# Hybrid decoder step on one core: first layer's token norms from rows of x, loads reordered, copies and small steps moved

## The chip, the cores and the metric

The kernel runs on one core of one Trainium2 chip. The metric is the device time of the whole program in microseconds (us), as a median of runs. Beside it stands one profiled execution, whose trace gives the rows below. TensorE is called PE here, its weight loads PEld, VectorE DVE, ScalarE ACT, GpSimd POOL and SyncE SP.

## The reference

Two layers of one mixer block over 512 prompt tokens and 8 sample tokens, width 1024, in float32:

```python
def mixer_layer(x, s0_re, s0_im, conv_buf, mk, mv, p):
    h = rmsnorm(x, p['norm_g'])
    u_a, z_a, u_b, z_b, q, z_x, g_a, g_b, g_x = jnp.split(h @ p['w_in'], IN_SPLITS, axis=-1)
    y_a, s_new = s5_branch(u_a, s0, ...)           # 32 groups x 64 complex states, scan over tokens
    ...                                            # GELU, half GLU, SiLU gate, projection: o_a
    v_b = u_b[..., :E_CONV] * jax.nn.sigmoid(u_b[..., E_CONV:])
    ...                                            # depthwise conv of 31, LayerNorm, gate: o_b
    ...                                            # attention into 256 memory tokens (mk, mv), gate: o_x
    m = jax.nn.sigmoid(g_a) * o_a + jax.nn.sigmoid(g_b) * o_b + jax.nn.sigmoid(g_x) * o_x
    x = x + (m @ p['w_out']).astype(x.dtype)
```

Here rmsnorm(x, g) is x * rsqrt(mean(x * x) + 1e-6) * g over the 1024 channels of a token. The memory keys and values mk, mv are rmsnorm(mem) @ w_k and @ w_v. A last rmsnorm ends the trunk, and states, conv buffers, keys and values are outputs too.

## The kernel before

The residual x lives transposed in SBUF as `xT` (channels on partitions, 8 tiles of 128 x 520: 512 prompt and 8 sample tokens in two halves of 260). Each engine has one hand-written program, in order, and semaphores tie them; `wait(eng, l, name, n)` waits in layer l for the n-th event of a name.

**Weights.** All of w_in, the branch weights and w_out pass through a ring of two slots `w_st` in 72 units of 512 KB a layer. For each unit SP issues a load (`ring_load`, L335), as soon as the slot's last unit has been split; ACT rounds it to `w_hi` (`high`, L1141), and the rest `w_lo` comes from a POOL subtraction (L613) or, for the units of `by_transfer`, from an ACT negation (L1140) and an adding DMA that POOL issues (L610). PE then makes three products per unit (`products`: L693 high by high, L699 the two mixed ones) into one of two PSUM accumulators `acc`, which ACT or DVE empties and frees (`acc_free`).

**Start.** SP issues, in this order: 11 small parameter rows (`parameter_rows`), two loads of memory rows `mrow`, the first of 8 key and value loads `kv_load` (three buffers `kvw`; load i from 3 on waits until load i-3 is used), the rows of x (`xrow`), two ring loads, 16 small state loads (`state_rows`), and then the other five kv_loads. PE turns parameters, memory rows and x rows (L658), makes keys and values in 8 steps (`key_values`, L735), and sums the squares of x over the channels with a matrix of ones (`sum_squares`, L748): ACT squares the 8 tiles of `xT` (L1099), DVE adds them up (L1569), PE sums over partitions, DVE scales and takes reciprocals over 128 x 520 (L1436, L1595), ACT the root (L1165) and `rs` is there. Then for each tile DVE scales it to `ht` (L1439), ACT rounds it to `h_hi` (L1168), DVE takes `h_lo` (L1601), and the first unit of layer 0 takes the tiles as they come.

**Inside a layer** PE goes through the units v, q, u, vb, zx, gx, zb, gb, za, ga, out, with attention, convolution (DVE, L1439), scans (DVE) and state products between them. What the change touches:
- `x_keep` stores xT to DRAM in four parts of 520 KB from SP's queue (L378), because `merge("gx", ...)` writes over xT; DVE waits for all four (`x_out`, L1874) before the first merge, and merges free the accumulators of the next gates (L1790).
- After the second scan `keep_states(1)` copies four blocks of X to X2 on DVE (L1843); PE's second state products (`outputs(1)`, L964) wait for it (L1845). In the first half DVE copies two blocks and ACT two (L1360).
- While the last 8 units of layer 0 (`out`) run, DVE adds each to xT (L1960), which frees its accumulator, and between them computes the next layer's state matrices: `powers` after the first add, `level_factors` after the second and third, and so on.

Of the kernel before, what the change touches and what calls it, by code (L numbers as in the profile page):

```python
# [21 lines left out]
P = 128  # L22
# [48 lines left out]
def build(nc, x_prompt, x_sample, mem_prompt, state_ssm_re, state_ssm_im, state_conv, cache_mem_k,  # L71
# [12 lines left out]
    with ctx:  # L84
# [54 lines left out]
        def rr(name, off, shape):  # L139
            return at(r_at, off, rlen, name, shape)  # L140
# [37 lines left out]
        msq = rr("msq", 7296, [P, D])  # L178
        kT = rr("kT", 6144, [P, HEADS, MEM])
# [74 lines left out]
            V2_done=2 X2_done=1 s_turned=2  # L254
# [10 lines left out]
        def wait(eng, l, name, value):  # L265

            eng.wait_ge(sm[name], l * per[name] + value)
# [50 lines left out]

        block = ctx.enter_context(nc.Block())
# [3 lines left out]
        def _(sp):  # L323
# [57 lines left out]
            def parameter_rows(l):  # L381
                sp.dma_start(dtrow[64:80, :], ssm_log_dt[l].rearrange("(q e) -> q e", e=2)).then_inc(sm["dt_in"], 16)
                rows = ((0, 16, ssm_a_re[l].rearrange("(q e) p -> q (e p)", e=2)),
                        (16, 4, b_glu[l].rearrange("(k p) -> k p", p=P)),
                        (20, 4, conv_b[l].rearrange("(k p) -> k p", p=P)),
                        (24, 4, conv_ln_g[l].rearrange("(k p) -> k p", p=P)),
                        (28, 4, conv_ln_b[l].rearrange("(k p) -> k p", p=P)),
                        (32, 16, ssm_a_im[l].rearrange("(q e) p -> q (e p)", e=2)),
                        (48, 8, norm_g[l].rearrange("(k p) -> k p", p=P)),
                        (56, 8, mem_norm_g[l].rearrange("(k p) -> k p", p=P)))  # L390
                for r0, n, src in rows:
                    sp.dma_start(prow[r0:r0 + n, :], src).then_inc(sm["p_in"], 16)
                sp.dma_start(cwrow[:, :], conv_w[l].rearrange("k (i c) -> (k i) c", c=P)).then_inc(sm["p_in"], 16)
                sp.dma_start(drow[:, :], ssm_d[l].rearrange("(q x) -> q x", x=P)).then_inc(sm["p_in"], 16)

# [44 lines left out]
            parameter_rows(0)  # L440
# [3 lines left out]
            kv_load(0, 0)  # L444
            kv_load(0, 1)
# [5 lines left out]
            sp.dma_start(xsrow[:, :], x_sample[:, 0, :]).then_inc(sm["xs_in"], 16)  # L451
            value_loads(0, "v", 0)
            state_rows(0)

            for l in range(LAYERS):
                for i in range(3, 8):
                    kv_load(l, i)
# [8 lines left out]
                in_loads(l, "q", 5 * E, 3, 4)  # L466
                cache_load(l, 1)
# [11 lines left out]
                if l == 0:  # L479
                    sp.wait_ge(sm["x_ev"], 5)  # L480
                else:
                    sp.wait_ge(sm["x_sum"], l * KT)
                x_keep(0, 2)
# [24 lines left out]
                x_keep(4, 6)  # L508
# [46 lines left out]
                if l + 1 < LAYERS:  # L555
                    wait(sp, l, "br_a_done", 4)
                    parameter_rows(l + 1)
# [98 lines left out]
        def _(pe):  # L656
# [122 lines left out]
            key_values(0, 4, 5)  # L779
# [5 lines left out]
            key_values(0, 5, 7)  # L785
            pe.wait_ge(sm["x_ev"], 5)
            sum_squares(0)
            key_values(0, 7, 8)
            state_parameters(0)

            for l in range(LAYERS):
# [155 lines left out]
                def outputs(f):  # L947
# [13 lines left out]
                    if f == 0:  # L961
                        wait(pe, l, "X2_done", 1)
# [128 lines left out]
        def _(act):  # L1091
# [18 lines left out]

            discretise(0)
# [13 lines left out]
            for i in range(4):  # L1125
# [16 lines left out]

            high(0)
            high(1)
            for l in range(LAYERS):
# [172 lines left out]

                gate("gx", 0)
# [38 lines left out]
                wait(act, l, "x_scan", 1)  # L1358
                for ri in range(2):
                    last = act.copy(X2[ri * S:(ri + 1) * S, :, 1, :], X[S:2 * S, ri, :, 0:YC])  # L1360
                last.then_inc(sm["X2_done"], 1)
# [10 lines left out]
                wait(act, l, "br_b_done", 4)  # L1372
                silu("za", 0, q)
# [54 lines left out]
        def _(dve):  # L1428
# [66 lines left out]
            def powers(l):  # L1495

                wait(dve, l, "par_act", 1)
# [3 lines left out]
                tt(pw[:, 1, :, 1], tiny[:, 3, :], tiny[:, 7, :], ALU.mult)  # L1501

# [13 lines left out]
                for lo in (1, 2, 4):  # L1516
                    a = tiny[:, 0:lo, :].rearrange("p k q -> p q k")
                    b = tiny[:, 4:4 + lo, :].rearrange("p k q -> p q k")
                    cmul(pw[:, 0, :, lo + 1:2 * lo + 1], pw[:, 1, :, lo + 1:2 * lo + 1], pw[:, 0, :, 1:lo + 1], pw[:, 1, :, 1:lo + 1],
                         pw[:, 0, :, lo:lo + 1].to_broadcast([P, Q, lo]), pw[:, 1, :, lo:lo + 1].to_broadcast([P, Q, lo]), a, b)  # L1520
# [66 lines left out]
            for k in range(1, KT):  # L1587
                add_square(0, k)
            steps.clear()

            for l in range(LAYERS):

                wait(dve, l, "sq_used", 1)
                ts(rs[:, :, :], mp[:, 0:2, 0:HC], 1.0 / D, EPS, ALU.mult, ALU.add)
                dve.reciprocal(rs[:, :, :], rs[:, :, :]).then_inc(sm["var_done"], 1)  # L1595

                wait(dve, l, "rstd_done", 1)

# [239 lines left out]
                def keep_states(f):  # L1838

                    qs = slice(f * QH, (f + 1) * QH)  # L1840
                    for e in range(f + 1):
                        for ri in range(2):
                            run(dve.tensor_copy(X2[ri * S:(ri + 1) * S, :, e, :], X[e * S:(e + 1) * S, ri, :, 0:YC]), behind=2 * e + ri)  # L1843
# [109 lines left out]
                merge("ga", 3)  # L1953
                steps.clear()

                for i in range(KT):
# [69 lines left out]
```

## Time and profile before

| | us |
|---|---|
| median of 3 runs (1249.85 to 1251.44) | 1251.43 |
| the profiled execution | 1245.38 |
| its span, first to last instruction | 1243.6 |
| PE busy in the span | 1119.2 |
| DVE busy | 729.0 |
| ACT busy | 479.8 |
| POOL busy | 245.1 |

The span lies 1.8 us below the time of its execution, and that execution 6.0 us below the median of the runs. Busy times overlap; a stage is read from the wait that ends last in it.

### The profile page before, as it was taken

Reading aid. Unit: us, or ns where it says so; the run is one execution under the profiler, and the core shown is the slowest. Engines: PE = TensorE matmul, PEld = TensorE weight load, DVE = VectorE, ACT = ScalarE, POOL = GpSimd, SP = SyncE. Lnnn points to the kernel's source line nnn. Section 1 sums busy time; section 2 is a strip of 40 time slices with the busy share of each in tenths; the row PEclk is TensorE's granted clock in tenths of the full one; section 3 lists DMA queues with packets and bytes.
Section 4 is the critical chain, followed back from the end, with each engine's and each line's share of the span. In section 5 each row is a group of like instructions: output and inputs, shape, how many; then the busy total and the mean of one; then the engine's idle time right before and its main releaser. Section 6 shows DMA issues by size and latency. Waiting matters only on the chain.

```text
span 1243.6 us, 20132 instructions
## 1 busy us (share of the span) xinstructions
PE 1119.2 (90%) x8266; PEld 1040.1 (84%) x8266; DVE 729.0 (59%) x1229; ACT 479.8 (39%) x646; POOL 245.1 (20%) x183
## 2 busy tenths in 40 slices
PE   5679999889999989998889999988999998899895
PEld 3359996788999979998865999678999898899895
DVE  4289965637678660545875766664557864133412
ACT  3233563434463622233123356343446362222112
POOL 0114111111110122243330411120111012124430
PEclk9779998989998998998899999898999898899998
DMA  8405878897765576173222588888876557424332
GB/s 234 118 12 162 215 200 241 221 154 155 171 136 122 137 158 120 57 231 117 64 88 85 149 224 205 237 228 150 168 156 135 124 139 156 90 66 138 108 109 76
DMA packets 217873, 181.98 MB, mean 146 GB/s; under 512 B 47146, under 2 KB 187882, under 8 KB 216998
## 3 DMA queue, kind: packets, MB, share of 16 engines
q1 hardware_dynamic: 205542, 135.61, 39.8%
q0 software_dynamic: 12096, 44.05, 19.4%
q8 instruction: 65, 1.06, 0.3%
q10 hardware_dynamic: 144, 1.05, 0.2%
q14 instruction: 26, 0.21, 0.1%
HBM read 121.86 MB, written 15.72 MB: 111 GB/s over the span
## 4 chain that ended last, share of the span: by engine, by line
PE 59%; DVE 17%; DMA 11%; SPq 6%; ACT 4%; issue 3%; DVEq 0%; POOL 0%; ACTq 0%
PE acc L699 31%; PE acc L693 15%; DMA w_lo<-w_st 5%; PE acc L1057 2%; DMA w_st<-in_w_in 2%; PE acc L735 2%; PE mp L964 2%; PE mp L658 1%; DVE cacc L1439 1%; ACT w_lo L1140 1%; SPq L514 1%; DVE xT L1433 1%; PE mp L929 1%; PE mp L832 1%; PE mp L867 1%
## 5 line engine op out<-in xcount | busy, mean ns | idle before, releaser
L699 PE MATMUL acc<-h_hi,w_lo 128*128 128x260 f32 x1664 | 341.0, 287 | 9.4 <-DMA w_lo<-w_st 9.4
L699 PE MATMUL acc<-h_lo,w_hi 128*128 128x260 f32 x1664 | 338.0, 285 | 0.0
L699 PEld LDWEIGHTS acc<-h_hi,w_lo 128*128 128x128 f32 x1664 | 261.0, 192 | 10.4 <-DMA w_lo<-w_st 10.4
L699 PEld LDWEIGHTS acc<-h_lo,w_hi 128*128 128x128 f32 x1664 | 261.0, 192 | 0.0
L1141 ACT CAST w_hi<-w_st 128x1024 fp32r<-128x1024 f32 x144 | 149.6, 1040 | 280.8 <-PE acc L699 244.3
L693 PE MATMUL acc<-h_hi,w_hi 128*128 128x260 f32 x1664 | 238.0, 297 | 19.3 <-DVEq L1602 10.9
L693 PEld LDWEIGHTS acc<-h_hi,w_hi 128*128 128x128 f32 x1664 | 219.3, 198 | 29.5 <-DVEq L1602 11.7
L613 POOL TENSOR_TENSOR w_lo<-w_st,w_hi 128x1024 fp32r<-128x1024 f32 x60 | 150.5, 2510 | 400.8 <-ACT w_hi L1141 400.8
L1140 ACT ACTIVATE w_lo<-w_st 128x1024 fp32r<-128x1024 f32 x84 | 89.1, 1060 | 304.9 <-PE acc L699 213.8
L610 POOL DMA_DIRECT2D w_lo<-w_st x84 | 73.0, 868 | 562.4 <-ACT w_lo L1140 552.8
L1439 DVE SCALAR_TENSOR_TENSOR cacc<-vx,cw,cacc 128x512 f32<-128x512 f32 x232 | 161.7, 767 | 3.6 <-DVE xT L1433 1.7
L699 PE MATMUL acc<-bh,w_lo 128*128 128x260 f32 x384 | 80.4, 292 | 9.6 <-DMA w_lo<-w_st 9.6
L1433 DVE TENSOR_TENSOR sg<-acc,sg 128x520 f32<-128x520 f32 x32 | 22.4, 699 | 111.5 <-PE acc L699 108.4
L735 PE MATMUL acc<-kvw,memg 128*128 128x512 f32 x128 | 62.6, 646 | 12.8 <-DMA kvw<-in_w_k 9.0
L699 PEld LDWEIGHTS acc<-bh,w_lo 128*128 128x128 f32 x384 | 62.0, 197 | 10.6 <-DMA w_lo<-w_st 10.6
L693 PE MATMUL acc<-bh,w_hi 128*128 128x260 f32 x384 | 58.0, 293 | 11.1 <-DVEq L1911 4.2
L735 PEld LDWEIGHTS acc<-kvw,memg 128*128 128x128 f32 x128 | 26.2, 209 | 44.3 <-issue 33.3
L693 PEld LDWEIGHTS acc<-bh,w_hi 128*128 128x128 f32 x384 | 51.5, 195 | 13.7 <-issue 5.3
L699 PE MATMUL acc<-m_hi,w_lo 128*128 128x260 f32 x256 | 54.9, 298 | 0.0
L699 PE MATMUL acc<-m_lo,w_hi 128*128 128x260 f32 x256 | 54.2, 295 | 0.0
L699 PE MATMUL acc<-q_r,w_hi 128*128 128x260 f32 x256 | 51.5, 283 | 0.0
L693 PE MATMUL acc<-m_hi,w_hi 128*128 128x260 f32 x256 | 36.3, 295 | 14.8 <-DVEq L1961 7.5
(282 smaller groups left out, 1397.4 us busy)
## 6 DMA issues: line engine op xcount, KB each, us to landing
w_st<-in_w_in SPq DMA_DIRECT2D x104, 512.0 KB, 4.7
w_lo<-w_st POOLq DMA_DIRECT2D x84, 512.0 KB, 5.5
kb<-in_cache_mem_k SPq DMA_DIRECT2D x16, 512.0 KB, 5.8
kb<-in_cache_mem_v SPq DMA_DIRECT2D x16, 512.0 KB, 7.0
w_st<-in_w_out SPq DMA_DIRECT2D x16, 512.0 KB, 4.0
x_scratch<-xT SPq DMA_DIRECT2D x8, 520.0 KB, 6.1
xT<-x_scratch SPq DMA_DIRECT2D x4, 1040.0 KB, 8.0
kvw<-in_w_k SPq DMA_DIRECT2D x8, 512.0 KB, 6.1
```

Of the source, the lines that this page charges most:

```text
L514: sp.dma_start(Ug[t * H:(t + 1) * H, :, NB:NB + C], ug[:, :, t // 4, (t % 4) * C:(t % 4 + 1) * C]).then_inc(sm["U_in"], 16)
L610: pool.dma_start(w_lo[:, n % 2, :], w_st[:, n % 2, :], accum_op=ALU.add).then_inc(w_lo_done[n % 2], 16)
L613: pool.tensor_tensor(w_lo[:, n % 2, :], w_st[:, n % 2, :], w_hi[:, n % 2, :].bitcast(F32), ALU.subtract).then_inc(w_sub_done, 1)
L693: pe.matmul(acc_ps[acc][:, a, 0:HC], w_of(w_hi, n % 2, k), high[:, k, a, :], start=(k == 0), stop=False)
L699: last = pe.matmul(acc_ps[acc][:, a, 0:HC], w_of(w, n % 2, k), x[:, k, a, :], start=False, stop=(k == kts - 1 and w is w_hi))
L735: last = pe.matmul(acc_ps[half][:, m, :], memg[:, k, m * P:(m + 1) * P], kvw[:, i % 3, kk * E:(kk + 1) * E], start=(k == 0), stop=(k == KT ...
L964: last = pe.matmul(mp[:, 2 * e + r // 4, (r % 4) * YC:(r % 4 + 1) * YC], V2[:, r, e, :], X2[:, r, e, :], start=False, stop=(r % 4 == 3))
L1057: last = pe.matmul(acc_ps[j][:, a, 0:HC], w_dir[:, g, k * 2 * P + j * P:k * 2 * P + (j + 1) * P], u[:, k, a, :], start=(k == 0), stop=(k = ...
L1140: act.activation(w_lo[:, n % 2, :], w_st[:, n % 2, :], ACT.Copy, scale=-1.0).then_inc(w_neg_done, 1)
L1141: act.copy(w_hi[:, n % 2, :], w_st[:, n % 2, :]).then_inc(w_hi_done, 1)
L1433: run(dve.tensor_tensor(out, a, b, op), behind)
L1439: run(dve.scalar_tensor_tensor(out=out, in0=a, scalar=s, in1=b, op0=op0, op1=op1), behind)
```

## The change

1. **Start, loads.** Five parameter rows are issued by ACT, six by SP, and these after the memory rows and the first kv_load. x_sample's rows are loaded after x's first block. kv_loads 3 to 5 come ahead of the state loads.
2. **Start, norm of layer 0.** ACT squares rows of x (and x_sample) with a sum over the row as it goes; DVE turns the five columns of sums into reciprocals and multiplies them into diagonal matrices `diag`, `sdiag`; PE multiplies ones by these, which spreads each token's value over all partitions; ACT takes the root from PSUM as `rs`. The squares of xT's tiles, their sums and the wide reciprocal of layer 0 go. PE turns x_sample's rows ahead of kv step 4 and makes the spread after it, where the sum came after step 6. PE turns the parameters after the first block of memory rows.
3. **x_keep** stands earlier in SP's order: the first part after unit q 3, the second where the first was, the others after vb and zx units.
4. **keep_states(1)** copies two blocks; ACT copies the other two (`states_turned(1)`), ahead of `silu("za", 0)`.
5. **powers** of layer 1 is cut in three, and the first two parts run ahead of the adds of `out`; a level moves from the second to the third add.

```diff
+        diag = rr("diag", 8320, [P, 4, P])
+        sdiag = rr("sdiag", 8832, [NB, NB])
...
 # SP
-            parameter_rows(0)
...
             kv_load(0, 0)
+            parameter_rows(sp, 0, 5)
             kv_load(0, 1)
...
                 if i == 0:
                     kv_load(0, 2)
-            sp.dma_start(xsrow[:, :], x_sample[:, 0, :]).then_inc(sm["xs_in"], 16)
+                    sp.dma_start(xsrow[:, :], x_sample[:, 0, :]).then_inc(sm["xs_in"], 16)
+            kv_load(0, 3)
             value_loads(0, "v", 0)
+            kv_load(0, 4)
+            kv_load(0, 5)
             state_rows(0)
...
-                for i in range(3, 8):
+                for i in range(3 if l else 6, 8):
...
                 in_loads(l, "q", 5 * E, 3, 4)
+                if l == 0:
+                    sp.wait_ge(sm["x_ev"], 5)
+                else:
+                    sp.wait_ge(sm["x_sum"], l * KT)
+                x_keep(0, 2)
                 cache_load(l, 1)
...
-                x_keep(0, 2)
+                x_keep(2, 4)
...
                 value_load(l, "vb", 3, 1)
-                x_keep(2, 4)
+                x_keep(4, 6)
                 in_loads(l, "zx", 6 * E, 0, 1)
+                x_keep(6, 8)
...
                 gate_loads(l, "gx", 2, 4)
-                x_keep(4, 6)
...
-                gate_loads(l, "gx", 4, 5)
-                x_keep(6, 8)
-                gate_loads(l, "gx", 5, 7)
+                gate_loads(l, "gx", 4, 7)
 # PE
-            parameters(0)
             for m in range(2):
                 pe.wait_ge(sm[f"mem_in{m}"], 16)
                 if m:
+                    parameters(0)
                     wait(pe, 0, "par_ev", 1)
...
-            key_values(0, 5, 7)
+            key_values(0, 4, 5)
             pe.wait_ge(sm["x_ev"], 5)
-            sum_squares(0)
-            key_values(0, 7, 8)
+            wait(pe, 0, "sq_summed", KT - 1)
+            for i in range(4):
+                pe.matmul(mp[:, i // 2, (i % 2) * P:(i % 2 + 1) * P], ones[:, :], diag[:, i, :], start=True, stop=True)
+            for a in range(2):
+                last = pe.matmul(mp[:, a, 4 * C:HC], ones[0:NB, :], sdiag[:, 4 * a:4 * a + 4], start=True, stop=True)
+            last.then_inc(sm["sq_used"], 1)
+            key_values(0, 5, 8)
...
-                    if f == 0:
-                        wait(pe, l, "X2_done", 1)
+                    wait(pe, l, "X2_done", f + 1)
 # ACT
+            parameter_rows(act, 0, 0, 5)
...
+            def square_row(i, rows, row):
+                act.wait_ge(sm["xs_in"] if i == 4 else sm[f"x_in{i}"], 16 if i == 4 else 32)
+                steps.run(act.activation(msq[0:rows, :], row, ACT.Square, accum_out=stat[0:rows, 16 + i:17 + i]))
+                act.sem_inc(sm["sq_done"], 4 if i == 4 else 1)
+
+            square_row(0, P, xrow[:, 0, :])
+            square_row(4, NB, xsrow[:, :])
+            for i in range(1, 4):
+                square_row(i, P, xrow[:, i, :])
...
-            for k in range(KT):
-                square(0, k)
...
                 if l == 0:
+                    wait(act, l, "sq_used", 1)
+                    act.activation(rs[:, :, :], mp[:, 0:2, 0:HC], ACT.Sqrt).then_inc(sm["rstd_done"], 1)
                     keep_keys(0, ktok)
-                    wait(act, l, "var_done", 1)
-                    act.activation(rs[:, :, :], rs[:, :, :], ACT.Sqrt).then_inc(sm["rstd_done"], 1)
...
                 wait(act, l, "br_b_done", 4)
+                states_turned(1)
                 silu("za", 0, q)
 # DVE
             powers(0)
-            for k in range(1, KT):
-                add_square(0, k)
+            wait(dve, 0, "sq_done", KT)
+            ts(stat[:, 21:25], stat[:, 16:20], 1.0 / D, EPS, ALU.mult, ALU.add, behind=1)
...
+            run(dve.reciprocal(stat[:, 26:30], stat[:, 21:25]), behind=1)
...
+            for i in range(4):
+                run(dve.tensor_scalar(diag[:, i, :], ident[:, :], stat[:, 26 + i:27 + i], None, ALU.mult), behind=i + 1)
+            run(dve.tensor_scalar(sdiag[:, :], ident[0:NB, 0:NB], stat[0:NB, 30:31], None, ALU.mult))
...
-                    for e in range(f + 1):
-                        for ri in range(2):
-                            run(dve.tensor_copy(X2[ri * S:(ri + 1) * S, :, e, :], X[e * S:(e + 1) * S, ri, :, 0:YC]), behind=2 * e + ri)
+                    for ri in range(2):
+                        run(dve.tensor_copy(X2[ri * S:(ri + 1) * S, :, 0, :], X[0:S, ri, :, 0:YC]), behind=ri)
...
                 merge("ga", 3)
+                if l + 1 < LAYERS:
+                    first_powers(l + 1)
+                    input_factors(l + 1)
...
-                            powers(l + 1)
+                            for lo in (1, 2, 4):
+                                more_powers(lo)
                         elif i == 1:
-                            level_factors(l + 1, 0, 3)
+                            level_factors(l + 1, 0, 2)
                         elif i == 2:
-                            level_factors(l + 1, 3, 5)
+                            level_factors(l + 1, 2, 5)
```

## Rows read from the trace of the kernel before

**Rows 1.** The page: engines' busy time; x_keep's DMAs (KB each, us to landing).

```profile
PE 1119.2 (90%) x8266; PEld 1040.1 (84%) x8266; DVE 729.0 (59%) x1229; ACT 479.8 (39%) x646; POOL 245.1 (20%) x183
...
x_scratch<-xT SPq DMA_DIRECT2D x8, 520.0 KB, 6.1
```

**Rows 2.** PE's waits, whole run: for whom, us in total, times, longest.

```profile
PE acc L735 <- DMA kvw<-in_w_k: 9.0, 1, 9.0
PE acc L693 <- DVEq L1790: 8.4, 3, 4.7
PE mp L964 <- DVEq L1845: 7.9, 2, 4.0
PE acc L693 <- DVEq L1961: 7.5, 3, 5.4
```

**Rows 3.** Timeline of the start: start us, us, instruction, [idle before <-releaser].

```profile
4.81 0.84 SPq L443 DMA_DIRECT2D mrow<-in_mem_prompt  x2
...
6.98 0.37 PE L658 MATMUL mp<-ident,prow 80*128 80x80 f32 x1 [6.98 <-DMA drow<-in_ssm_d]
...
8.14 3.86 PE L658 MATMUL mp<-ident,mrow 128*128 128x128 f32 x16 [0.39 <-DMA mrow<-in_mem_prompt]
...
14.53 8.80 PE L735 MATMUL acc<-kvw,memg 128*128 128x512 f32 x16 [2.53 <-DVE memg L1580]
...
14.66 1.06 ACT L1119 ACTIVATE msq<-mrow 128x1024 f32<-128x1024 f32 x1
...
24.04 3.60 PE L735 MATMUL acc<-kvw,memg 128*128 128x512 f32 x8
...
51.03 9.73 DVE L1569 TENSOR_TENSOR sq<-sq 128x520 f32<-128x520 f32 x7 [23.85 <-ACT sq L1099]
...
67.25 0.64 ACT L1165 ACTIVATE rs<-rs 128x520 f32<-128x520 f32 x1 [2.85 <-DVE rs L1595]
```

**Rows 4.** The chain that ended last, whole run: start us, us, what.

```profile
33.48 4.03 DMA kvw<-in_w_k
...
82.72 5.75 PE acc L699 x32
...
90.38 3.83 PE acc L699 x32
...
465.59 6.92 PE mp L964 x32
...
983.95 3.76 PE mp L964 x32
```

**Rows 5.** PE, timeline around the first merges of layers 0 and 1.

```profile
259.24 1.91 PE L658 MATMUL mp<-ident,wt 128*128 128x128 f32 x16
265.88 3.81 PE L693 MATMUL acc<-h_hi,w_hi 128*128 128x260 f32 x16 [4.73 <-DVEq L1790]
...
856.41 3.81 PE L693 MATMUL acc<-h_hi,w_hi 128*128 128x260 f32 x16 [3.55 <-DVEq L1790]
```

**Rows 6.** ACT there in layer 0; then stretches: us, busy by engine, PE clock, DMA share, GB/s.

```profile
265.58 1.92 ACT L1287 COPY wl<-mp 128x1024 f32<-128x1024 f32 x2
...
105.00:110.00 5.00, 5.00 (x44) 5.00 (x43) 4.52 (x15) 1.66 (x4) 2.21 (x1) 1.00 0.70 212
...
15.00:20.00 5.00, 5.00 (x9) 2.11 (x8) 2.89 (x18) 4.03 (x7) 0.00 (x0) 0.66 1.05 313
```

**Rows 7.** DVE, timeline of the adds of out, layer 0 (columns as in rows 3).

```profile
590.15 0.70 DVE L1433 TENSOR_TENSOR xT<-acc,xT 128x520 f32<-128x520 f32 x1 [6.83 <-PE acc L699]
...
591.41 2.53 DVE L1433 TENSOR_TENSOR pw<-tiny 128x16 f32<-128x16 f32 x2
...
596.79 0.41 DVE L1433 TENSOR_TENSOR tiny<-pw 128x16 f32<-128x16 f32 x2
```

**Rows 8.** Copies to X2 in layer 0, and POOL's subtractions beside them, by timeline.

```profile
459.20 5.98 DVE L1843 COPY X<-X 64x576 f32<-64x576 f32 x4
...
459.32 5.06 POOL L613 TENSOR_TENSOR w_lo<-w_st,w_hi 128x1024 fp32r<-128x1024 f32 x2 [8.41 <-ACT w_hi L1141]
```

More of the change, by code:

```diff
@@ L317, in g3, with parameter_rows @@
             return ap[:, :, :, 0:4 * C]
+        def parameter_rows(eng, l, first=0, end=11):
+            if first == 0:
+                eng.dma_start(dtrow[64:80, :], ssm_log_dt[l].rearrange("(q e) -> q e", e=2)).then_inc(sm["dt_in"], 16)
+            rows = ((0, 16, ssm_a_re[l].rearrange("(q e) p -> q (e p)", e=2)),
+                    (16, 4, b_glu[l].rearrange("(k p) -> k p", p=P)),
+                    (20, 4, conv_b[l].rearrange("(k p) -> k p", p=P)),
+                    (24, 4, conv_ln_g[l].rearrange("(k p) -> k p", p=P)),
+                    (28, 4, conv_ln_b[l].rearrange("(k p) -> k p", p=P)),
+                    (32, 16, ssm_a_im[l].rearrange("(q e) p -> q (e p)", e=2)),
+                    (48, 8, norm_g[l].rearrange("(k p) -> k p", p=P)),
+                    (56, 8, mem_norm_g[l].rearrange("(k p) -> k p", p=P)))
+            for r0, n, src in rows[max(first - 1, 0):end - 1]:
+                eng.dma_start(prow[r0:r0 + n, :], src).then_inc(sm["p_in"], 16)
+            if end < 11:
+                return
+            eng.dma_start(cwrow[:, :], conv_w[l].rearrange("k (i c) -> (k i) c", c=P)).then_inc(sm["p_in"], 16)
+            eng.dma_start(drow[:, :], ssm_d[l].rearrange("(q x) -> q x", x=P)).then_inc(sm["p_in"], 16)
         block = ctx.enter_context(nc.Block())
@@ L1124, in _, with high @@
             act.wait_ge(sm["mem_rt"], 1)
+            def high(n):
+                if n < LAYERS * UNITS:
+                    act.wait_ge(w_loaded[n % 2], (n // 2 + 1) * 16)
+                    if by_transfer(n):
+                        act.activation(w_lo[:, n % 2, :], w_st[:, n % 2, :], ACT.Copy, scale=-1.0).then_inc(w_neg_done, 1)
+                    act.copy(w_hi[:, n % 2, :], w_st[:, n % 2, :]).then_inc(w_hi_done, 1)
+            def square_row(i, rows, row):
[6 more added lines that the diff above has]
+                square_row(i, P, xrow[:, i, :])
             for i in range(4):
@@ L1130, in _ @@
             act.activation(xT[:, :, :, 4 * C:HC], mp[:, 0, 0:KT * NB].rearrange("p (k a c) -> p k a c", a=2, c=4), ACT.Copy).then_inc(sm["x_ev"], 1)
-            for k in range(KT):
-                square(0, k)
             steps.clear()
-            def high(n):
-                if n < LAYERS * UNITS:
-                    act.wait_ge(w_loaded[n % 2], (n // 2 + 1) * 16)
-                    if by_transfer(n):
-                        act.activation(w_lo[:, n % 2, :], w_st[:, n % 2, :], ACT.Copy, scale=-1.0).then_inc(w_neg_done, 1)
-                    act.copy(w_hi[:, n % 2, :], w_st[:, n % 2, :]).then_inc(w_hi_done, 1)
             high(0)
@@ L1317, in turned_outputs, with states_turned @@
                     last.then_inc(sm["V2_done"], 1)
+                def states_turned(f):
+                    wait(act, l, "x_scan", f + 1)
+                    for ri in range(2):
+                        last = act.copy(X2[ri * S:(ri + 1) * S, :, 1, :], X[S:2 * S, ri, :, 0:YC])
+                    last.then_inc(sm["X2_done"], 1)
                 gate("gx", 0)
@@ L1357, in _ @@
                 gate("gb", 2)
-                wait(act, l, "x_scan", 1)
-                for ri in range(2):
-                    last = act.copy(X2[ri * S:(ri + 1) * S, :, 1, :], X[S:2 * S, ri, :, 0:YC])
-                last.then_inc(sm["X2_done"], 1)
+                states_turned(0)
                 gelu_outputs(0)
@@ L1840, in keep_states @@
                     qs = slice(f * QH, (f + 1) * QH)
-                    for e in range(f + 1):
-                        for ri in range(2):
-                            run(dve.tensor_copy(X2[ri * S:(ri + 1) * S, :, e, :], X[e * S:(e + 1) * S, ri, :, 0:YC]), behind=2 * e + ri)
+                    for ri in range(2):
+                        run(dve.tensor_copy(X2[ri * S:(ri + 1) * S, :, 0, :], X[0:S, ri, :, 0:YC]), behind=ri)
                     run(dve.tensor_copy(sf[:, :, qs], X[:, :, :, XC - 1]))
@@ L1964, in _ @@
                         if i == 0:
[L1965 removed]
+                            for lo in (1, 2, 4):
+                                more_powers(lo)
                         elif i == 1:
[L1967 removed]
+                            level_factors(l + 1, 0, 2)
                         elif i == 2:
[L1969 removed]
+                            level_factors(l + 1, 2, 5)
                         elif i == 3:
```

49 lines of the change are left out of this document (20 added, 29 removed).

## The prediction

> **What bounds the kernel now.** I read the page first: PE is busy for 1119 of 1243.6 us [rows 1], so a gain can only come from stretches where PE stands still or runs at its lower clock. The list of PE's waits gives the places [rows 2]: a key load at the start, the merges of gx (L1790), the second state products (L964), the adds of `out` (L1961). The timeline of each place gives the size. At the start PE sets little: the fourth key step waits for a load that was issued at 33.48 only, behind the small state loads [rows 4], and the norm of x is a long chain of DVE work (7 adds over 9.73 us, later a wide reciprocal) before the root at 67.25 [rows 3]; layer 0's first unit ends at 82.72 + 5.75 = 88.5 [rows 4]. By then the 8 key steps, at 3.6 us when PE doesn't wait [rows 3], could have been over for 30 us. The reader is to see that this stretch is set by order, not by work.
>
> **Edits 1 and 2, the start.** I work out when the first unit ends.
>
> Keys begin at 14.53 now, when both blocks of memory rows are turned, copied and scaled [rows 3]. Their loads were issued at 4.81 and the first was there at 8.14, 3.3 us later; they now go out first, at about 0.7. But PE turns the parameters ahead of the second block, and six parameter rows are issued behind two memory blocks and a key load, 1.5 MB. At the 313 GB/s of a full stretch [rows 6] 512 KB take 1.7 us, so in order of issue these rows land at 0.7 + 3.3 + 2 x 1.7 = 7.4 plus their own 1 to 2.5 us, against 6.98 now [rows 3]. Taken at 8.9, with an estimated 1.6 us for their turns and copies (6.98 to 8.14 is 1.2, and a little is left after it) and the 4.4 us from the second block's turns (halfway through the 3.86 us after 8.14, at 10.1) to 14.53, keys begin at 14.9. Were the rows to land as soon as now after their issue (2.6 us after some 4 us of issues), keys would begin at 12.5; the other bound is 16.5, with all of the queue ahead of them and 2.6 us more. I take 15.0, since no row shows a small load passing a large one.
>
> The Trainium skill ("DMA: Bandwidth & Descriptors", Queues, rings and completion order) says that a DMA engine takes the descriptors of one ring in order, which speaks against putting parameters behind 1.5 MB: by it 15.0, and 1202.9 at the end; without it 12.5 and 1200.4. The same page (Issuing engines are not separate DMA queues) says that the five rows on ACT save issue time alone. No row of this trace shows a parameter load on ACT's queue.
>
> From there PE's order is: two key steps and x block 0, 9.5 us (14.53 to 24.04); key step 2, 3.6; x block 1, 1.0 (half of a memory block's 1.9, which ran at the lower level); step 3, 3.6; two x blocks, 2.0; x_sample 0.7 (estimate, smaller than a block); step 4, 3.6; the spread, 0.9 (estimate; from 0.4, half a block, to 2) [rows 3]. That is 24.9, so the root starts at 39.9 instead of 67.25.
>
> From the root to the end of the high products 15.5 us pass now (67.25 to 82.72), bound by DVE's two steps per tile, and they stay. The next steps on ACT, two copies of keys, fall in DVE's first tile and cost some 0.2. But POOL's two first subtractions now fall about here: one that meets a DVE step costs it 2.1 us (two steps took 2.53 at 591.41 and the same two 0.41 at 596.79 [rows 7]). I take 1.3, between 0 and 2.1. High products then end at 56.7. By PE's count alone (three more key steps from 39.9) it would be free at about 52, so the tiles decide. The mixed products take 3.83 after a busy PE and 5.75 after a waiting one [rows 4]; I take 4.6: 61.3. **Gain 27.2**, bounds 19 (keys at 16.5, spread 2, collision 2.1, 5.75, a key load late by its 4.0) and 32.
>
> The Trainium skill ("SBUF — State Buffer", Who interferes with whom) has the rule for the collision: VectorE with two SBUF inputs and a GpSimd step that reads SBUF lock each other out for a whole instruction. By it the term is up to a whole subtraction, 2.5 us (5.06 for two in [rows 8]) instead of 1.3, and the sum 1.2 us later.
>
> At nothing I cost: the five row squares on ACT, 5 x 1.25 (1.06 [rows 3] and an estimated 0.2 for the sum), from about 20 to 27, hidden because PE asks for the first x copy at 15 + 9.5 + 3.6 + 1.0 + 3.6 = 32.7 (uncovered, up to 6 us); DVE's nine small steps, done by about 30, asked for at 39; the key loads. Load 3 is issued when step 0 is over, at 19.4, lands in 4.0 and is wanted at 29; SP waits there, and behind it stand the ring loads, which ACT wants only at 36. Loads 6 and 7 come after the state loads, as load 3 did; I see about 2 us of slack, and a late one costs at most 4.0 [rows 4].
>
> **Edit 3, the stores.** PE stands still before gx's third gate for 4.73 and 3.55 us, since DVE's first merge waits for the last store, and the gate's first block then runs in 3.81 [rows 5]. A block's 16 products at the higher level take half, 1.9, so 1.9 more goes each time. Gone: 6.6 in layer 0, 5.4 in layer 1. Next late are ACT's `wl` copies, over at 267.5 [rows 6]; the gate would run from 261.2 (259.24 + 1.91) for 1.9 + 3.83 to 266.9, so the state products wait half a microsecond, not seven. On SP the third and fourth stores leave the place ahead of U's loads and the ring loads of gx, and all parts now go ahead of loads in the q, vb and zx units. There the DMA engines are busy to 0.70 (105 to 110) [rows 6], so a store fits; bounds are 0 and 1.7 us (520 KB at 313 GB/s) for three stores a layer, 10 in all. I take 1.0, near the first, by the free share. **Gain 11.0**, bounds 2 and 12.
>
> **Edit 4, X2.** DVE's four copies in layer 0 take 5.98 beside POOL's two subtractions [rows 8]; PE waits 7.9 us in the two layers [rows 2], and the products after it take 6.92 instead of 3.76 [rows 4]. With two copies left, the second still meets POOL's first subtraction in layer 0 and ends at about 462.3, 3.0 earlier; if PE's pause then is short enough, up to 3.2 more. In layer 1 one copy pair saves 1.0; and ACT now does its copies before it splits unit za 2, so POOL's subtraction of that unit comes after the scan and 2.1 of collision leave it. Bounds are 1.0 and 6.2 in each layer; I take 3.0 and 4.0. The new wait on ACT for the scan holds `silu("za", 0)`, that split and the GELU tables; PE wants them after its state products and unit za 1, over 9 us later (3.76 + 5.75), so it is hidden; uncovered it costs what the scan is late. What follows, y through DRAM, starts with the products and moves with them. **Gain 7.0.**
>
> **Edit 5, powers.** DVE sits idle for 6.83 us before the first add [rows 7]. The steps from 591.4 to 596.8, 5.4 us, move into that pause. 2.1 of them are a collision, which meets another step instead, since POOL still has one subtraction per unit and DVE stays the bound. **Gain 3.3**, bounds 1.5 and 5.4. The level that goes to the third add is the same work.
>
> **Sum.** 27.2 + 11.0 + 7.0 + 3.3 = 48.5: the profiled 1245.4 would be 1196.9, and, as that execution lies 6.0 below the median of the runs, the median 1202.9.
>
> **Rivals.** *The start pays less*, because a load is late: parameters behind still more of the queue, or keys behind ring loads of many short rows. For it speaks that SP's order is the whole edit and that a key load was the longest wait; against it the slack above. With 8 us lost the time is 1211. *The stores give nothing*: the merge goes earlier, but state products wait for U's loads or `wl`, late by the same DMAs. For it speaks 267.5 being only 0.6 after 266.9; against it that x's stores leave that stretch. Gain 2 instead of 11: 1212. *Slower*: the stores move into the stream of weights, and each delays a unit by its whole landing, 6.1 us [rows 1]. Eight of them cost 49 and edit 3 gives nothing: 1251.4 - 37.5 + 49 = 1263. It decides from 37.5 / 8 = 4.7 us a store; against it the DMA share of 0.70, and that one store stood among the vb units already. *Nothing happens*: the norm isn't what the first unit waits for; the rows at 67.25 and 82.72 speak against it.
>
> **Numbers.** Forecast 0.72, less at the start 0.12, no gain from the stores 0.11, slower 0.02, nothing 0.02, the rest between. The range takes in the first two rivals on one side and most of the good bounds (32 + 12 + 10 + 5 = 59) on the other: 1191 to 1219. A measurement of this kernel tells some 0.2%, 2.5 us, from no change: faster 0.96, same 0.02, slower 0.02.
>
> **What would show it.** Layer 0's first mixed products near 57 instead of 82.7, the root near 40, no wait of PE for a key load. No wait of PE for L1790 before gx's third gate, and that block in 1.9. L964's wait under 1.5 us at least once. The add of tile 6 some 3 us sooner after the add of tile 0. Wrong I'd be if keys began past 18, if PE's waits for `w_lo` or `w_st` grew by more than 10 us in the q to zx units, or if PE's mean clock fell.

## The result: 1200.9 us, 0.959 of the time before

The changed kernel takes 1200.88 us (median of 4 runs, 1198.69 to 1206.69) against 1251.43 before; the ratio is 0.9594, 95% interval 0.9553 to 0.9636. A second set of six runs, beside experiments below, gave 0.9623 (0.9593 to 0.9652). Where a single part is taken away I compare with the mean of the two, 0.961, good to some 0.0025 (3 us). The profiled execution takes 1202.02 us, 43.4 less than the one of before; its mean granted clock is 0.963 instead of 0.944. The second set has a profiled execution too (1199.59 us), called the second execution below. The forecast was 1203, and 48.5 us of gain.

### The profile after

The page's rows for the engines' busy time and for the stores answer to [rows 1]:

```profile
PE 1107.5 (92%) x8274; PEld 1032.2 (86%) x8274; DVE 713.0 (59%) x1225; ACT 483.1 (40%) x652; POOL 246.6 (21%) x183
...
x_scratch<-xT SPq DMA_DIRECT2D x8, 520.0 KB, 5.3
```

PE's waits over the whole run (for whom, us in total, times, longest) answer to [rows 2]:

```profile
PE acc L706 <- DMA w_lo<-w_st: 23.6, 12, 4.4
PE acc L700 <- DVEq L1841: 6.9, 2, 3.5
...
PE acc L700 <- DVEq L2007: 4.9, 3, 2.7
...
PE mp L974 <- ACT X L1342: 3.6, 4, 1.3
```

The key load is gone from the list, and so is L1834 (L1790 before), the merge that frees an accumulator. L974 holds all state products: the second ones, which waited 7.9 us for VectorE, have 2.3 of its 3.6, now for ScalarE. L2007 (the adds of `out`) is down from 7.5 to 4.9. L1841 (L1797 before, 7.3 us) is the end of the last merge, for which the first unit of `out` waits in each layer (the first at 553); it has changed little. The row for `w_lo`, a weight's low part that a DMA makes, was 18.9 before: some of the gain goes there.

The start, by the timeline, answers to [rows 3, 4]:

```profile
0.74 0.88 SPq L447 DMA_DIRECT2D mrow<-in_mem_prompt  x2
...
8.54 0.37 PE L665 MATMUL mp<-ident,prow 80*128 80x80 f32 x1 [2.14 <-DMA drow<-in_ssm_d]
...
14.67 9.16 PE L742 MATMUL acc<-kvw,memg 128*128 128x512 f32 x16 [2.54 <-DVE memg L1614]
...
28.84 3.60 PE L742 MATMUL acc<-kvw,memg 128*128 128x512 f32 x8
...
40.19 0.60 ACT L1183 ACTIVATE rs<-mp 128x520 f32<-128x520 f32 x1 [2.90 <-PE mp L797]
...
55.29 0.40 PE L706 MATMUL acc<-h_hi,w_lo 128*128 128x260 f32 x2
...
59.13 1.13 PE L700 MATMUL acc<-h_hi,w_hi 128*128 128x260 f32 x8
```

The root starts at 40.19 instead of 67.25. Mixed products run from 55.29 to 59.13 (the next unit's start), 3.84 us, where before they ran from 82.72 for 5.75: the first unit is over 29 us sooner.

How the lead grows and shrinks is seen by taking the same instruction of PE in the profiles of both kernels (starts in us; the last row is the span; the last column is the lead of the second execution):

| instruction | before | after | lead | lead, second execution |
|---|---|---|---|---|
| second unit, layer 0 (the first is over) | 88.31 | 59.13 | 29.2 | 27.9 |
| first unit behind the first softmax | 154.36 | 128.17 | 26.2 | 26.8 |
| products of U, layer 0 (behind gx's third gate) | 274.10 | 240.57 | 33.5 | 33.6 |
| first glu product, layer 0 (behind y) | 492.82 | 461.69 | 31.1 | 31.2 |
| keys of layer 1 (`out` is over) | 642.24 | 606.16 | 36.1 | 34.9 |
| products of U, layer 1 | 864.62 | 823.70 | 40.9 | 39.4 |
| first glu product, layer 1 | 1088.64 | 1046.26 | 42.4 | 45.9 |
| end | 1243.6 | 1200.2 | 43.4 | 45.8 |

So the lead falls in two stretches: up to the first softmax, by 3.0 in one execution and 1.1 in the other, and between the products of U and glu in layer 0, by 2.4 in both, although the state copies of edit 4 lie in that stretch. In the others it grows or holds.

**The first softmax.** Timelines of VectorE (end of the first unit's tiles; the first probabilities) and of PE there, after:

```profile
54.98 0.42 DVE L1497 COPY s<-mp 128x256 f32<-128x256 f32 x1
...
122.68 1.22 DVE L1457 TENSOR_TENSOR pr<-pr,stat 128x1024 f32<-128x1024 f32 x1
...
124.02 1.44 PE L665 MATMUL mp<-ident,pr 128*128 128x128 f32 x8 [1.87 <-DVEq L1676]
125.25 3.27 PE L843 MATMUL mp<-kT,q 128*128 128x256 f32 x8
```

and before:

```profile
81.95 0.42 DVE L1473 COPY s<-mp 128x256 f32<-128x256 f32 x1
...
149.35 1.22 DVE L1433 TENSOR_TENSOR pr<-pr,stat 128x1024 f32<-128x1024 f32 x1
...
151.95 1.03 PE L658 MATMUL mp<-ident,pr 128*128 128x128 f32 x8
152.82 1.89 PE L832 MATMUL mp<-kT,q 128*128 128x256 f32 x8
```

VectorE needs 67.4 us from the tiles to the probabilities before (149.35 - 81.95) and 67.7 after: it works for 64 of them, through state inputs, level factors and a convolution. Its own lead is 27.0, PE's was 29.2; PE waits 1.87 for it and its next eight products then take 3.27 instead of 1.89. The lead above VectorE's is gone. In the second execution PE comes as VectorE is done, and both the wait and the slow products are missing:

```profile
125.05 1.09 PE L665 MATMUL mp<-ident,pr 128*128 128x128 f32 x8
125.98 1.89 PE L843 MATMUL mp<-kT,q 128*128 128x256 f32 x8
```

The products of U stand at 240.57 in the one and at 240.48 in the other. So a loss of this size belongs to one execution, and by the products of U it is no longer seen.

**The stores, state copies and adds.** PE at gx's third gate and its products of U in layer 0, and at the gate in layer 1 [rows 5]:

```profile
234.20 2.15 PE L700 MATMUL acc<-h_hi,w_hi 128*128 128x260 f32 x16
...
240.57 3.76 PE L940 MATMUL mp<-U,wl 128*128 128x72 f32 x32 [0.38 <-ACT wl L1306]
...
817.87 2.16 PE L700 MATMUL acc<-h_hi,w_hi 128*128 128x260 f32 x16
```

No wait and no slow block. The state copies and products in layer 0, and the products in layer 1 [rows 8]:

```profile
433.41 1.36 ACT L1342 COPY X<-X 64x576 f32<-64x576 f32 x2 [7.46 <-DVEq L1880]
...
433.41 0.94 DVE L1886 COPY X<-X 64x576 f32<-64x576 f32 x2
...
434.91 6.78 PE L974 MATMUL mp<-X,V 128*128 128x72 f32 x32 [1.28 <-ACT X L1342]
...
1018.74 6.91 PE L974 MATMUL mp<-X,V 128*128 128x72 f32 x32 [1.05 <-ACT X L1342]
```

The copies run side by side on two engines and end 1.4 us after the scan; the wait is 1.28 and 1.05 us, but the products still run slowly, 6.78 and 6.91 (6.44 and 5.71 in the second execution) instead of the 3.76 of a stretch at the upper clock [rows 4]. VectorE's adds of `out` for tiles 0 and 6, after [rows 7]:

```profile
557.50 0.70 DVE L1457 TENSOR_TENSOR xT<-acc,xT 128x520 f32<-128x520 f32 x1 [0.80 <-PE acc L706]
...
605.35 0.70 DVE L1457 TENSOR_TENSOR xT<-acc,xT 128x520 f32<-128x520 f32 x1
```

Before, tile 6 was added at 641.43, 51.3 after tile 0; now it is 47.9. The idle time ahead of the first add shrank from 6.83 to 0.80: the moved steps fill it.

### The profile page after: what moved, and what is told of

Its sections match the earlier page's. It is cut to its first block, busy times and chain, and to the rows that moved or that the text cites. A ratio compares the mean times of both kernels' runs of the same rounds, so it can differ in the third digit from the quotient of the medians.

```text
span 1200.2 us, 20152 instructions
## 1 busy us (share of the span) xinstructions
PE 1107.5 (92%) x8274; PEld 1032.2 (86%) x8274; DVE 713.0 (59%) x1225; ACT 483.1 (40%) x652; POOL 246.6 (21%) x183
## 4 chain that ended last, share of the span: by engine, by line
PE 53%; DVE 18%; DMA 14%; ACT 4%; SPq 3%; issue 2%; DVEq 0%; POOL 0%; ACTq 0%
PE acc L706 28%; PE acc L700 13%; DMA w_lo<-w_st 8%; DMA w_st<-in_w_in 4%; DVE cacc L1463 3%; PE acc L1067 2%; PE mp L974 2%; DVE wt L1457 2%; ACT w_lo L1142 2%; DVE tiny L1457 1%; PE mp L665 1%; PE acc L742 1%; PE mp L878 1%; PE mp L843 1%; DMA y_scratch<-U 1%
## 5 line engine op out<-in xcount | busy, mean ns | idle before, releaser
L700 PE MATMUL acc<-h_hi,w_hi 128*128 128x260 f32 x1664 | 231.8, 292 | 4.4 <-DVEq L1646 4.4
L700 PEld LDWEIGHTS acc<-h_hi,w_hi 128*128 128x128 f32 x1664 | 214.8, 194 | 12.7 <-issue 6.4
L742 PE MATMUL acc<-kvw,memg 128*128 128x512 f32 x128 | 58.5, 613 | 3.6 <-DVE memg L1614 2.5
L706 PE MATMUL acc<-m_lo,w_hi 128*128 128x260 f32 x256 | 52.2, 286 | 0.0
```

The lines of the kernel that those rows point to most:

```text
L700: pe.matmul(acc_ps[acc][:, a, 0:HC], w_of(w_hi, n % 2, k), high[:, k, a, :], start=(k == 0), stop=False)
L706: last = pe.matmul(acc_ps[acc][:, a, 0:HC], w_of(w, n % 2, k), x[:, k, a, :], start=False, stop=(k == kts - 1 and w is w_hi))
L742: last = pe.matmul(acc_ps[half][:, m, :], memg[:, k, m * P:(m + 1) * P], kvw[:, i % 3, kk * E:(kk + 1) * E], start=(k == 0), stop=(k == KT ...
```

## The experiments

All ratios are to the kernel before, run alongside; in brackets their 95% intervals. Each kernel but two starts from the changed one.

### Start alone, the rest alone

The kernel before with edits 1 and 2 only.

> The kernel before with the new start alone (edits 1 and 2). As predicted: 1251.4 - 27.2 = 1224 us, with layer 0's first unit over at about 59 us of the span. Rival, PE's gain is cut by VectorE's own backlog at the first softmax (there the changed kernel waits 1.9 us and runs slow after it, and its lead falls from 31.2 to 26.0 us): the end shows about 25 to 26, that is 1226. Rival, the start pays some 8 less: 1232.

Measured: 0.9799 [0.9772, 0.9827], a gain of 25.2 us. That excludes the start paying 8 less and can't tell 27.2 from 25 or 26; PE's first transposes of probabilities stand at 123.76 there, no sooner than in the changed kernel (124.02), but hardly wait:

```profile
123.76 1.09 PE L666 MATMUL mp<-ident,pr 128*128 128x128 f32 x8 [0.28 <-DVEq L1677]
124.69 1.89 PE L844 MATMUL mp<-kT,q 128*128 128x256 f32 x8
```

PE's lead over the kernel before is 27.8 at the second unit and 28.1 behind the softmax, so the rival's 25 to 26 may be the time, but its mechanism is not seen in this profile. The lead goes later: it is 28.0 at the products of U and 22.7 at the first glu product, for PE waits 3.80 us at 421 for the `w_lo` of gb's last unit (0.93 before) and 2.47 for y from DRAM (0.95 before). The lead of 31.2 in the expectation should be the 29.2 of the table. The rest alone, on the old start (edits 3 to 5):

> The kernel before with its old start and with the moves of stores, state copies and powers (edits 3 to 5). As predicted: 1251.4 - 21.3 = 1230 us. If the parts help each other (the start's lead is partly lost at the first softmax without them), start only and rest only sum to less than the 50.6 us of both; if one hides the other they sum to more.

Measured: 0.9829 [0.9803, 0.9855], a gain of 21.4 us, the forecast being 21.3. The sum of both, 46.6, stands beside 48.9 for both at once (0.039 of 1253), give or take 6: no sign that the halves help or hide each other.

### Stores back

```diff
-                x_keep(0, 2)
...
-                x_keep(2, 4)
...
+                x_keep(0, 2)
...
-                x_keep(4, 6)
+                x_keep(2, 4)
...
-                x_keep(6, 8)
...
                 gate_loads(l, "gx", 2, 4)
+                x_keep(4, 6)
...
-                gate_loads(l, "gx", 4, 7)
+                gate_loads(l, "gx", 4, 5)
+                x_keep(6, 8)
+                gate_loads(l, "gx", 5, 7)
```

> The changed kernel with the stores of x alone put back to their old places. As predicted (edit 3 is worth 11.0): about 1212 us, and PE stands still again for some 4 us before gx's third gate in both layers, with that gate's first block in 3.8 us. Rival, the stores give nothing because other loads are late anyway: 1203 (2 us). Rival, the two stretches are worth what they show in the traces (gains of 8.0 and 9.9 us around the third gate) and the stores cost nothing where they stand now: 1219. If the stores slow the weight loads they now stand among, PE's waits for w_lo (23.6 us in the changed kernel) fall by some us here.

Measured: 0.9727 [0.9693, 0.9761], 14.6 us (give or take 5) slower than 0.961; the profiled execution, 1212.2, is 10.2 above that of the changed kernel. PE's timeline has the two waits and the two slow blocks again:

```profile
237.79 3.81 PE L701 MATMUL acc<-h_hi,w_hi 128*128 128x260 f32 x16 [4.51 <-DVEq L1835]
...
828.37 3.80 PE L701 MATMUL acc<-h_hi,w_hi 128*128 128x260 f32 x16 [4.43 <-DVEq L1835]
```

So "the stores give nothing" is out; the forecast's 11 and the 18 of the third theory both lie within the interval. By the timelines of PE, the stretch from the first unit behind the softmax to layer 0's products of U takes 119.8 us here and 112.4 and 113.0 in the changed kernel's two executions, and that from the keys of layer 1 to its products of U 224.6 against 217.5 and 217.9: some 7 us in each layer, 14 in all. `w_lo`'s waits fall to 18.2 us, which could mean that the stores slow those weights where they stand now. The next kernel tests that.

### Stores of 4 KB

```diff
-                sp.dma_start(x_dram[:, first * w:end * w],
...
+                sp.dma_start(x_dram[:, first * w:first * w + 8],
+                             xT[:, first, 0, 0:8]).then_inc(sm["x_out"], 16)
```

> The changed kernel with stores of x of 8 columns of one tile each, in the same places with the same waits, and with what is read back taken from the weights in place of the stored x: it leaves out the bytes of the residual. If the stores cost what was predicted where they stand now (1.0 us for all): 1200 us, w_lo's waits unchanged at 23 us. If they are behind the growth of PE's waits for w_lo from 18.9 to 23.6 us: 1196 us, with some 5 us less of these waits.

Measured: 0.9615 [0.9577, 0.9653], the changed kernel's own time, and the row of PE's waits is where it was:

```profile
PE acc L706 <- DMA w_lo<-w_st: 23.2, 12, 4.0
```

The time alone, good to some 6 us, can't exclude the second theory's 5; the row does: without the bytes the waits are the same. The bytes of eight stores, 4 MB, cost nothing that can be measured here. The changed kernel beside it:

> The changed kernel once more, beside the three others of this group: 1201 us (1197 to 1206).

Measured: 0.9623 [0.9593, 0.9652], 1207.82 us (1199.59 to 1209.01), with 21.6 us of waits for `w_lo`. The median lies just outside what I wrote; the kernel before was 1254.63 in this group.

### The halves of the start

The changed kernel with the old norm (edit 2 undone):

> The changed kernel with edit 2 undone: the new load order with the old norm (squares of the turned tiles, seven adds of VectorE, a wide reciprocal). By the prediction's steps x is turned at 35, the squares end near 44, the adds near 46 and the root comes 6.5 us behind them as before, at 52.6 instead of 40.2: 12.4 us later than the changed kernel, 1213 us. Rival, the order of the loads carries the whole gain: 1201 to 1203. Rival, the norm carries nearly all of it: 1222 or more.

Measured: 0.9696 [0.9672, 0.9719], 10.8 us slower than 0.961 (give or take 4). With the old order of the loads instead (edit 1 undone):

> The changed kernel with edit 1 undone: the old load order with the new norm. Key load 3 stands behind the state loads again and lands near 37.5 where PE wants it at 28.8; the spread stands behind that key step, so the root comes 8.7 us later, at 49: 1210 us. Rival, the norm carries the whole gain: 1201 to 1203. If both parts are needed, the two alone leave less of the 27 us than their sum: 14.8 and 18.5.

Measured: 0.9726 [0.9696, 0.9756], 14.5 us slower (give or take 5). Root of the first, then key step 3 and root of the second, by the timeline:

```profile
51.88 0.64 ACT L1178 ACTIVATE rs<-rs 128x520 f32<-128x520 f32 x1 [2.85 <-DVE rs L1623]
```

```profile
40.80 5.66 PE L739 MATMUL acc<-kvw,memg 128*128 128x512 f32 x8 [10.48 <-DMA kvw<-in_w_k]
...
54.20 0.60 ACT L1179 ACTIVATE rs<-mp 128x520 f32<-128x520 f32 x1 [2.90 <-PE mp L794]
```

The first came as worked out (52.6 forecast). In the second the key load lands 3.3 us later than forecast and its step then runs slowly (5.66 instead of 3.60), so the root is at 54 and not at 49. Each half carries a part of the start, and neither the whole. The loads' order alone leaves 25.2 - 10.8 = 14.4 us and the norm alone 25.2 - 14.5 = 10.7, together 25.1: no sign that one needs the other.

### State copies back, powers back

```diff
 # ACT
-                states_turned(1)
...
 # DVE
-                    for ri in range(2):
...
+                    for e in range(f + 1):
+                        for ri in range(2):
```

> The changed kernel with edit 4 undone: VectorE makes all copies of the states. As predicted 7.0 us slower than the changed kernel (3.0 in layer 0, 4.0 in layer 1), that is 0.967 to 0.968 of the kernel before, and PE waits again near 4 us for VectorE before each second state product. Rival, ScalarE's copies only take the wait over: under 2 us.

Measured: 0.9664 [0.9638, 0.9691], 6.8 us slower (give or take 5). PE's second state products:

```profile
435.60 7.07 PE L975 MATMUL mp<-X,V 128*128 128x72 f32 x32 [3.90 <-DVEq L1889]
...
1026.76 7.07 PE L975 MATMUL mp<-X,V 128*128 128x72 f32 x32 [4.12 <-DVEq L1889]
```

The waits of before are back, 2.6 and 3.1 us longer than with ScalarE's help. For the powers `first_powers` and `input_factors` go back behind the first add:

> The changed kernel with edit 5 undone: the powers in one piece behind the first add. As predicted 3.3 us slower, 1.5 to 5.4, and the add of tile 6 comes 3 us later behind the add of tile 0. Rival, nothing: the memory keys of layer 1 start when their loads and scaled rows are there, and an earlier end of the adds is lost before them.

Measured: 0.9607 [0.958, 0.9633]. In time nothing is seen; the interval allows up to some 4 us. The timeline shows the edit at its place, the adds of tiles 0 and 6 standing 51.4 us apart instead of 47.9:

```profile
558.59 0.70 DVE L1457 TENSOR_TENSOR xT<-acc,xT 128x520 f32<-128x520 f32 x1 [7.00 <-PE acc L706]
...
609.94 0.70 DVE L1457 TENSOR_TENSOR xT<-acc,xT 128x520 f32<-128x520 f32 x1
```

PE's keys of layer 1 move with the adds: they start 52.2 us behind tile 0's add (at 610.76), 48.7 in the changed kernel (at 606.16). So the rival's reason is out, though the time doesn't show the 3.5 us.

### The wait at the first softmax

```diff
-                    level_factors(0, 0, 5)
...
                 convolution(2, 0, c1)
+                if l == 0:
+                    level_factors(0, 0, 5)
```

> The changed kernel with layer 0's level factors (12.9 us of VectorE from 74.0 to 86.9) moved behind the four softmaxes. If VectorE's backlog is what holds the first softmax, PE's wait of 1.9 us at 124 and the 1.6 us lost at the lower clock after it are gone: some 3 to 5 us sooner than the changed kernel, 1196 to 1198. Rival, the weights' loads or ScalarE end last there anyway: 1200 to 1201, with a wait for w_lo or for an accumulator in place of the one for VectorE.

Measured: 0.9616 [0.9589, 0.9642]: no gain is seen, and up to 4 us are not excluded. PE in u's first unit, at the softmax, and at the first glu product:

```profile
106.86 0.51 PE L706 MATMUL acc<-h_hi,w_lo 128*128 128x260 f32 x2 [2.02 <-DMA w_lo<-w_st]
...
124.48 1.04 PE L665 MATMUL mp<-ident,pr 128*128 128x128 f32 x8
125.35 1.89 PE L843 MATMUL mp<-kT,q 128*128 128x256 f32 x8
...
461.76 4.70 PE L1067 MATMUL acc<-u,w_dir 128*128 128x260 f32 x10 [2.53 <-DMA u<-y_scratch]
```

VectorE has the probabilities ready 5.5 us before PE comes, so its backlog is out of the way. But PE comes no sooner, at 124.48 against 124.02 and 125.05 in the changed kernel's two executions; it has waited 2.02 us for a `w_lo`, as the rival says (1.11 and 2.10 there). The products run in 1.89, which they also do in the second execution without this edit. And the glu product, which needs y back from DRAM, starts at 461.76, where the changed kernel has 461.69 and 461.60, after waits for that DMA of 2.53, 0.50 and 2.33 us. So whatever is won at the softmax is gone by glu.

### Two units split by GpSimd

```diff
-  return unit["q"] + 2 <= n % UNITS < unit["za"]
+  return unit["q"] + 2 <= n % UNITS < unit["za"] and n % UNITS not in (unit["gx"] + 1, unit["gb"] + 11)
```

> The changed kernel with two weight units a layer (gx unit 1 and gb unit 11) split by GpSimd's subtraction instead of the transfer that PE waits for (3.2 and 3.8 us in layer 0, 2.8 and 4.4 in layer 1). If the lead over the loads is what ends last there, PE's waits for w_lo fall from 23 to some 10 us and the kernel gains 6 to 10 us: 1192 to 1195. Rival, the next unit's weight is late by the same DMAs or the subtractions slow VectorE: under 3 us.

Measured: 0.9512 [0.9485, 0.9538], 1194.18 us: 12 us (give or take 5) better than the changed kernel, and the best of all. PE's waits for `w_lo`, and the one near gx:

```profile
PE acc L706 <- DMA w_lo<-w_st: 14.3, 9, 3.2
```

```profile
209.35 0.51 PE L706 MATMUL acc<-h_hi,w_lo 128*128 128x260 f32 x2 [3.21 <-DMA w_lo<-w_st]
```

The waits for gb's last unit, 3.78 us at 418 and 4.38 at 1002 (3.75 and 2.20 in the second execution), are gone, and no other took over at their place; y's way through DRAM cost more, though (6.9 us of waits in all, 1.7 and 4.5 before the edit). The second state products behind them took 5.13 and 3.76, so some more may have come from the clock. Whether the whole gain is that of this unit is not shown, for both units were changed at once. In gx I had the wrong unit: PE still waits there, so the late transfer is that of unit 0. Whether splitting that one pays more was not tried.

The same kernel with the late factors, and with all parameter rows on ScalarE's queue:

> The kernel with two units split by GpSimd, layer 0's level factors behind the softmaxes, and all parameter rows on ScalarE's queue. If a queue's own order held the six rows back, they land 2.6 us after their issue, near 7.8 instead of 8.5, and keys start some 0.7 us sooner; if the DMA engines' order holds them wherever they are issued, they land at 8.5 or later. In time 3 us below the kernel with the two units alone if the softmax's wait counts at the end, the same if the transfer of y through DRAM takes it back.

Measured: 0.9576 [0.9552, 0.96], 8 us worse than the two units alone. The timeline shows why (the last row's issue; the parameters and the keys on PE):

```profile
5.49 0.69 ACTq L337 DMA_DIRECT2D drow<-in_ssm_d  x1
...
19.21 0.37 PE L664 MATMUL mp<-ident,prow 80*128 80x80 f32 x1 [13.08 <-DMA drow<-in_ssm_d]
...
25.33 9.44 PE L741 MATMUL acc<-kvw,memg 128*128 128x512 f32 x16 [2.54 <-DVE memg L1613]
```

The rows were there 13 us after their issue, and keys begin at 25.33 instead of 14.67. By 5.49 SP had issued 3.0 MB (memory, three key loads, the first block of x). Another 1.5 MB, the other blocks of x, followed. Up to 19.0 us the two queues had moved (packets, MB, busy share; q1 is SP's queue, q10 ScalarE's):

```profile
q1 hardware_dynamic: 1677, 4.51, 90.7%
q10 hardware_dynamic: 296, 0.10, 3.3%
```

That is more than the 3.0 MB, so most of what was issued later went ahead of the rows too. Both of my theories fail: a queue of its own neither lets the rows pass nor keeps them in the order of issue. At the end the kernel has made up for some of the 10.7 us; how much of that the late factors give stays open.

## Why the prediction was right

**Start, 27.2 forecast.** Measured 25.2 in time (22 to 29), 29.2 at the first unit's end. Keys 15.0, found 14.67; root 39.9, found 40.19; mixed products 56.7, found 55.29, since GpSimd's two subtractions were over by 41.1, when VectorE's tiles had hardly begun: the 1.3 us for the collision were not paid. They took 3.84, not 4.6. Nine profiles, those of the experiments included, have this start: keys begin at 14.67 to 16.08 (so the bound of 12.5, rows that pass large loads, is out), the mixed products take 3.84 or 5.37, and the second unit starts at 59.1 to 60.7 instead of the forecast's 61.3, a lead of 27.6 to 29.2. So the steps came as worked out. Two slips carry no weight: the 0.2 us for the copies of keys is not in the 56.7, and the bound of 16.5 for the keys is 16.0 by the numbers given for it (7.4 + 2.6 + 1.6 + 4.4).

What I had put at nothing is what becomes of the lead behind the first unit. VectorE's backlog of setup, 67 us long, meets PE at the first softmax; it takes back 3.0 us in the profiled execution, 1.1 in the second and none with the start alone. More goes before layer 0's glu, 5.3 us with the start alone, where the `w_lo` of gb's last unit and y are late next. Against the time of the kernel these are small, so the sum holds; that it holds to 2 us is partly luck.

**Stores, 11.0.** Measured 14.6 (10 to 19) in time and 10.2 in the profiled executions. Both waits and both slow blocks went, as counted, and the lead grows by 7.3 and 4.8 us over these stretches (6.6 and 5.4 forecast); the block takes 2.15, not 1.9. That the stores fit beside the weights was chosen by the free share of the DMA engines; the kernel with stores of 4 KB bears it out. PE's waits for `w_lo` grew by 4.7 us, under the 10 that I gave as a sign of failure; in the q to zx units they did not grow (3.2 before, 3.0 after), and the bytes of the stores are not behind them.

**State copies, 7.0.** Measured 6.8 (2 to 11). The waits fall by 2.8 us in each layer, and the last is under 1.5 as foreseen. The forecast had 3.0 and 4.0; the 4.0 holds 0.9 more than its two terms (1.0 and 2.1). The products after them took 6.9 and 7.1 us before, 6.78 and 6.91 in the profiled execution and 6.44 and 5.71 in the second, so little came of the up to 3.2 that I left to the bound.

**Powers, 3.3.** Seen as 3.4 us between the adds; PE's keys of layer 1 follow tile 0's add 3.5 us sooner, too. In time the run with them back can't tell 3.3 from nothing.

**Sum.** 25.2 + 14.6 + 6.8 and about nothing for the powers is 46.6; the two measurements of the whole give 49 (46 to 52), the forecast 48.5. The profiled executions show 43.4 only, that of before lying 6.0 below its median and that of after 1.1 above. In it, terms that were paid were partly given back: 3.0 at the softmax, and 2.4 by glu in layer 0, where gb's last unit waits 3.78 us for its `w_lo` instead of 0.93. The second execution shows 45.8, with 1.1 and 2.4 given back at these places.

## What to carry to other kernels

When a chain at the start is shortened, look on every other engine for the queue that was hidden behind it, and compare leads instruction by instruction, in more than one execution: at the first softmax one execution of the same kernel lost 3.0 us and the other 1.1. Put loads in order of use on whatever queue: here eleven small rows on a queue of their own were there 13 us after the last issue, while 4.5 MB moved on the other. Once stalls are gone, the next bound is in the list of waits already: one line that changes who splits two weight units a layer gave 12 us more, a quarter of what the whole change gave.

## What the runs showed of the hardware

- Small loads behind large ones: with 1.5 MB issued ahead the six rows were there 4.1 us after the last issue (4.47 to 8.54); from ScalarE's queue, beside 3.0 MB issued and 1.5 MB still to come, 13 us (6.18 to 19.21). The Trainium skill ("DMA: Bandwidth & Descriptors", Issuing engines are not separate DMA queues) says that DMAs of all issuing engines run on the same 16 DMA engines and that a second issuer saves issue time alone; these traces agree (4.51 MB of SP's queue moved meanwhile), and show that it can cost far more than it saves.
- Eight stores of 520 KB put between weight loads did not lengthen PE's waits for weights (23.2 us without their bytes, 21.6 and 23.6 with them).
- After a pause of 1.0 to 1.4 us PE's clock fell in most cases, but not in all. Stretches of the changed kernel (us, busy time by engine, granted clock, DMA share, GB/s): the state products in layers 0 and 1 after pauses of 1.28 and 1.05 us, then the products of U after 0.38; last, from the kernel with two units split by GpSimd, the state products in layer 1 after 1.19:

```profile
434.90:441.40 6.50, 6.49 (x32) 6.50 (x33) 3.88 (x8) 4.11 (x4) 2.42 (x1) 0.53 0.01 3
1018.70:1025.50 6.80, 6.76 (x33) 6.80 (x33) 3.90 (x8) 4.13 (x4) 2.42 (x1) 0.52 0.01 2
240.60:244.20 3.60, 3.60 (x33) 3.60 (x33) 0.00 (x0) 3.23 (x4) 0.86 (x1) 1.00 0.72 137
...
1009.00:1012.70 3.70, 3.70 (x33) 3.70 (x34) 3.49 (x7) 3.65 (x4) 2.42 (x1) 1.00 0.30 88
```

Granted were 0.53 and 0.52, that is about the lower level of 1.2 GHz, and 1.00, the upper one. In all fourteen profiles of this case, 32 state products took 3.76 us each time after a pause of 0.63 (28 cases), 3.76 to 7.07 after pauses of 1.04 to 1.39 (21 cases, 3.76 once), and 6.9 to 7.1 after 3.9 to 4.1 (6 cases). So a wait of little more than a microsecond can cost up to three more behind it, which is why the state copies gave so little of what I left to the bound.
